# A hybrid decoder layer on one core: weight-quarter sums one product sooner, four low halves one step later, and three small steps moved inside the mixer

## The reference

```python
f = lb + (1.0 - lb) * jax.nn.sigmoid(rf)           # lb: lower bounds, a softmax over two rows
k = 1.0 - f; q = silu(rq)
o, S_new = _hgrn2_scan(q, log(f), k, ri, S0)       # S <- f*S + k i ; o = q S
p = exp(s - m) / (sum(exp(s - m)) + exp(sink - m)) # attention probabilities
x = x + _rmsnorm(concat(attention, o * silu(rg)) @ w_out, g_post_mix)
ffn = (silu(h2 @ w_gate) * (h2 @ w_up)) @ w_down   # 1024 -> 2816 -> 1024
x = x + _rmsnorm(ffn, g_post_ffn)
```

## Time and profile before

| | us |
|---|---|
| median of 3 runs | 1178.89 (1178.26 to 1178.94) |
| the profiled execution | 1179.54 |
| its span, first to last instruction | 1177.8 |
| PE busy | 1165.0 (99% of the span) |
| DVE busy | 874.2 (74%) |
| ACT busy | 533.7 (45%) |
| POOL busy | 242.2 (21%) |

### The profile page before, as it was taken

How to read it: one execution, slowest core, us unless ns; L and a number is a source line. 1 busy time by engine, 2 the same in 40 slices (tenths; PEclk the granted TensorE clock), 3 DMA queues, 4 the chain that set the end, 5 groups by cost and what they waited for, 6 DMA issues and landing times.

```text
span 1177.8 us, 22993 instructions
## 1 busy us (share of the span) xinstructions
PE 1165.0 (99%) x8962; PEld 1147.4 (97%) x8962; DVE 874.2 (74%) x1493; ACT 533.7 (45%) x1192; POOL 242.2 (21%) x190
## 2 busy tenths in 40 slices
PE   9999999999999999999999999999999999999998
PEld 9999999999999999999999999999999999999997
DVE  4988587776677747799777888888887565567676
ACT  6766656745253744564222322322322235455533
POOL 1000010201120000000232365765674020000011
PEclk9999999999999999999999999999999999999999
DMA  9521101006562243253454648766864286678446
GB/s 298 144 84 34 37 19 39 19 3 125 53 157 81 84 152 94 73 158 93 138 157 153 193 162 251 234 225 224 251 233 162 101 271 189 211 255 272 147 103 118
DMA packets 173548, 170.65 MB, mean 145 GB/s; under 512 B 23064, under 2 KB 125224, under 8 KB 172912
## 3 DMA queue, kind: packets, MB, share of 16 engines
q1 hardware_dynamic: 171264, 166.00, 46.8%
q0 software_dynamic: 2176, 3.18, 1.8%
HBM read 117.59 MB, written 52.58 MB: 144 GB/s over the span
## 4 chain that ended last, share of the span: by engine, by line
PE 86%; DVE 7%; ACT 3%; issue 2%; DMA 1%; SPq 0%; DVEq 0%; ACTq 0%
PE pair L2069 33%; PE pair L2109 17%; PE pair L1811 16%; PE pair L2028 7%; PE pair L1940 2%; PE pair L1886 1%; PE pair L2171 1%; PE pair L1901 1%; PE pair L1905 1%; DMA mix<-x_cols_dram 1%; DVE w_lo L2594 1%; PE pair L1925 1%; DVE mix L2666 1%; DMA raw<-w_in_dram 1%; PE pair L1957 1%
## 5 line engine op out<-in xcount | busy, mean ns | idle before, releaser
L2069 PE MATMUL pair<-act_hi,w_hi 128*128 128x258 f32 x704 | 199.1, 283 | 1.1 <-DVE u_tmp L2744 1.1
L2069 PE MATMUL pair<-act_lo,w_hi 128*128 128x258 f32 x704 | 198.6, 282 | 0.0
L2069 PE MATMUL pair<-act_hi,w_lo 128*128 128x258 f32 x704 | 198.6, 282 | 0.0
L2109 PE MATMUL pair<-a_ring,w_hi 128*128 128x258 f32 x1056 | 191.6, 284 | 0.5 <-DVE mix L2804 0.4
L1811 PE MATMUL pair<-act_hi,w_hi 128*128 128x344 f32 x528 | 177.0, 335 | 0.6 <-DVE act_lo L2242 0.5
L1811 PE MATMUL pair<-act_hi,w_lo 128*128 128x344 f32 x528 | 169.2, 320 | 0.0
L1811 PE MATMUL pair<-act_lo,w_hi 128*128 128x344 f32 x528 | 168.9, 320 | 0.0
L2109 PEld LDWEIGHTS pair<-a_ring,w_hi 128*128 128x128 f32 x1056 | 163.1, 189 | 1.5 <-DVE mix L2804 0.8
L1261 ACT ACTIVATE w_hi<-rawx 128x512 fp32r<-128x512 f32 (+2 forms) x97 | 68.7, 709 | 195.9 <-PE pair L2069 84.6
L2069 PE MATMUL pair<-s_hi,w_hi 128*128 128x258 f32 x528 | 149.2, 283 | 0.5 <-DVE w_lo L2594 0.5
L2069 PE MATMUL pair<-mix_r,w_hi 128*128 128x258 f32 x528 | 149.3, 283 | 0.0
(11 more groups left out here) (382 smaller groups left out, 2629.1 us busy)
## 6 DMA issues: line engine op xcount, KB each, us to landing
raw<-w_up_dram SPq DMA_DIRECT2D x26, 512.0 KB, 5.2
a_in<-h_sums SPq DMA_DIRECT2D x44, 258.0 KB, 3.3
rawx<-w_gate_dram SPq DMA_DIRECT2D x22, 512.0 KB, 5.1
w_quarter<-w_down_dram SPq DMA_DIRECT2D x44, 256.0 KB, 3.7
w_sums<-w_quarter SPq DMA_DIRECT2D x44, 256.0 KB, 4.7
rawx<-w_sums SPq DMA_DIRECT2D x44, 256.0 KB, 4.0
raw<-w_in_dram SPq DMA_DIRECT2D x18, 512.0 KB, 4.1
h_scratch<-mix SPq DMA_DIRECT2D x23, 258.0 KB, 2.1
```

The source lines that it names most:

```text
L2069: mm = pe.matmul(pair[psum_pair(n)][:, s, 0:QW], a[:, r, half + k, :], b, start=(k == 0 and i == 0), stop=(k == 3 and i == 2))
L2109: mm = pe.matmul(dpair(mt)[:, s, 0:a.shape[1]], b[:, cut], a, start=(m == 0 and n == 0), stop=(m == HALVES - 1 and n == 2))
```

## The change

Five edits; nothing is computed otherwise.

- The steps `L` of the four row sums move by one place: the first from n = 11 to 12 (behind `Y` of tile 0), the second from 12 to 13, the third from 13 to 15 (behind `Z`), the fourth from 15 to 16, behind `T4` and `W` of tile 0. The order among the four sums stays.
- For the tiles 1 to 7, `T` moves from iteration -3, where `Y` stays, to -4, counted from the tile's P6.
- The lower bounds are cut in two: three DVE instructions behind `D` of tick 27, the exponential on ACT at the end of tick 28's attention, the other five on DVE at tick 29, and a change of sign of one gain vector at tick 31.
- `R` of the one attention item that meets tick 70 moves on ACT to the end of tick 69, ahead of `unit_read`.
- On level 4 (the fifth) of heads 0 and 1, at ticks 60 and 78, DVE does the level first and `unit_finish` behind it.

```diff
 early_steps
-            8: [("S", 1, 1), ("S", 3, 1)], 9: [("X", 6), ("S", 2, 1), ("S", 4, 1)], 10: [("X", 7)], 11: [("T", 0), ("L", 2)],
-            12: [("Y", 0), ("L", 1)], 13: [("L", 3)], 14: [("T3", 0)], 15: [("Z", 0), ("L", 4)]}.get(n, [])
+            8: [("S", 1, 1), ("S", 3, 1)], 9: [("X", 6), ("S", 2, 1), ("S", 4, 1)], 10: [("X", 7)], 11: [("T", 0)],
+            12: [("Y", 0), ("L", 2)], 13: [("L", 1)], 14: [("T3", 0)], 15: [("Z", 0), ("L", 3)]}.get(n, [])
 weight_steps
-            plan = {-3: ("T", "Y"), -1: ("T3", "Z"), 0: ("T4", "W")} if q else {0: ("T4", "W")}
+            plan = {-4: ("T",), -3: ("Y",), -1: ("T3", "Z"), 0: ("T4", "W")} if q else {0: ("T4", "W")}
 shared
+    def scaled_early(tick):
+        return any(("o", h) in recurrence_steps(tick - 2) for h in range(NREC))
 scalar (ACT)
-            if tick == LB0:
-                act.wait_ge(sem("lb_step"), 1)
-                act.activation(lbt[:, 2:4, :], lbt[:, 0:2, :], ACT.Exp).then_inc(sem("lb_step"), 1)
-                elif step == "R":
+                elif step == "R" and not scaled_early(tick):
+            if tick == LB0 + 1:
+                act.wait_ge(sem("lb_step"), 1)
+                act.activation(lbt[:, 2:4, :], lbt[:, 0:2, :], ACT.Exp).then_inc(sem("lb_step"), 1)
+                    if step == "R" and scaled_early(tick + 1):
+                        unit_probabilities(i)
                 unit_read(tick // 2)
+            if n == 2 * EARLY:
+                sum_high(4)
 vector (DVE)
-        def lower_bound():
+        def bound_exponents():
             dve.wait_ge(sem("const_in"), NCONST)
             then(dve.tensor_tensor(lbt[:, 4, :], lbl[:, 0, :], lbl[:, 1, :], ALU.max))
             dve.tensor_tensor(lbt[:, 0, :], lbl[:, 0, :], lbt[:, 4, :], ALU.subtract)
             dve.tensor_tensor(lbt[:, 1, :], lbl[:, 1, :], lbt[:, 4, :], ALU.subtract).then_inc(sem("lb_step"), 1)
+
+        def lower_bound():
+
             dve.wait_ge(sem("lb_step"), 2)
-            if tick == LB0:
-                lower_bound()
-                dve.wait_ge(sem("g_in"), 16)
-                then(dve.tensor_scalar(gain[:, PRE_FFN, :], gain[:, PRE_FFN, :], -1.0, None, ALU.mult))
+            if tick == LB0:
+                bound_exponents()
+            if tick == LB0 + 2:
+                lower_bound()
+            if tick == LB0 + 4:
+                dve.wait_ge(sem("g_in"), 16)
+                then(dve.tensor_scalar(gain[:, PRE_FFN, :], gain[:, PRE_FFN, :], -1.0, None, ALU.mult))
-            levels_first = any(step[0] == "level" and step[1] >= NREC - 2 for step in recurrence_steps(tick))
+            levels_first = any(step[0] == "level" and (step[1] >= NREC - 2 or step[2] == 4) for step in recurrence_steps(tick))
+            if n == 2 * EARLY:
+                sum_low(4)
```

## The result

The changed kernel takes 1181.33 us (median of 20 runs, 1180.02 to 1182.87) against 1179.26 for the kernel before (20 runs, 1177.86 to 1181.57). The ratio is 1.0016, 95% interval 1.0010 to 1.0022 (it is not the quotient of the two medians): a little slower, by about the 0.2% that the prediction set as its bound. The forecast was 1179.8, 0.9 more than before, and too little to be told from no change. The interval leaves 1.0000 out, so 20 runs of each do tell it. The profiled execution took 1181.03 us, its span is 1179.2; the granted clock is 0.998 as before.

A forecast was written before the change was run, and what follows sets the result against it. PE is busy 99% of the span, so only its own waits count. Terms -0.30 - 0.26 + 1.15 + 0.8 - 0.45 = +0.94 us on the median 1178.89 gave 1179.8, own range 1179.0 to 1180.7, wide 1177.2 to 1181.4.

The forecast's parts named there:

- rival 4: Behind PE's new wait of 1.9 us at P3 the clock falls, costing 1.7 us: 1181.5 us; chance 0.07.
- Lower bounds: Ticks 27 to 31: DVE instructions moved behind the maximum end PE's wait at tick 28; gain 0.30, bounds -0.3 and +0.3.
- Scaling: Moving R on ACT ends PE's 0.56 wait at the transpose; -0.26 taken, the rest lost at head 1's levels.
- the 0.82: PE's level wait at 236.49 in head 1, 0.82 us, claimed to grow above 1 by the rest of the scaling gain.
- Level 4: Heads 0 and 1: unit_finish behind the level makes DVE 0.76 late; +0.4 for head 0, +0.75 for head 1.
- Low halves: Feed-forward products: u_tmp's 1.1 wait goes, but the fourth sum delays P3 to 553.7, losing 1.9; +0.8 taken.
- Weight sums: Tiles 2, 4 and 6: Y is ready some 0.7 sooner in each, ending tile 7's 0.45 wait; -0.45 taken.
- third rival: Odd tiles: POOL's instructions hold T, so PE's wait at tile 7 stays; 1180.3 us, chance 0.10.
- Rival 1: All four targeted PE waits go and nothing comes in their place: 2.5 us gained, 1176.4 us; chance 0.12.
- rival 2: Level 4 of heads 0 and 1: the order costs nothing, the shift falls into idle time; 1178.7 us, chance 0.18.

The follow-up runs named there:

- experiments 1: The changed kernel with the order of the row sums' low halves put back, all else kept: 1179.23 us, ratio 1.0003 to the kernel before.
- 2: The changed kernel with the level test put back, so unit_finish stands ahead of level 4 again: 1178.99 us, ratio 0.9996 to the kernel before.
- 6: The kernel before with only the level edit (level ahead of unit_finish at level 4 of heads 0 and 1): 1180.52 us, ratio 1.0012.
- the repeat: The changed kernel, unaltered, timed once more: 1181.70 us, ratio 1.0023 to the kernel before.
- experiments 3: The third order: the changed kernel with low halves of the third sum ahead of Z, the fourth ahead of T4 and the reading before it: 1178.73 us, ratio 0.9998.
- 4: The changed kernel with the level test put back and the low halves in the third order: 1177.09 us, ratio 0.9982 to the kernel before.

## Why the prediction was right, point by point

The sum was +0.94 and the columns give +1.03 (without the start and the stretch that no edit touches). That the two are so near is partly luck: three terms were 30 to 43% too small, two of them gains (0.52 together) and one a loss (0.49). And the median is not as near as the sum: 1181.33 lies above the forecast's own range (1179.0 to 1180.7), at the end of the wide one (1181.4), next to rival 4's 1181.5, though the clock didn't fall behind P3. Of the 1.5 us between it and 1179.8, 0.37 is that the kernel before had 1179.26 in 20 runs and 1178.89 in the three of the forecast; most of the rest is in no term and no column ("What stays open"). So that it still lies in the wide range is luck; what came out is the mechanism of each edit but one, and their sum in the traces.

- **Lower bounds**, forecast -0.30, measured -0.53. The mechanism was right. The size was not: the listed wait is not all that PE loses at it (below).
- **Scaling**, forecast -0.26, measured -0.25: right in size by luck, wrong in place. "The rest is added to the 0.82" failed. PE wins 0.78 at the transpose and gives 0.38 and 0.14 back at two score matmuls ahead of the level, in ticks 72 and 76. In the changed kernel:

```profile
213.93 0.19 ACT L1460 ACTIVATE esk<-tsum 128x2 f32<-128x2 f32 x1
...
214.15 0.16 DVE L2458 TENSOR_TENSOR den<-den,esk 128x2 f32<-128x2 f32 x1 [3.94 <-ACT esk L1460]
...
215.41 0.31 PE L1818 MATMUL pair<-act_hi,w_lo 128*128 128x344 f32 x1
215.55 0.16 DVE L2454 TENSOR_TENSOR tsum<-sink,negm 128x2 f32<-128x2 f32 x1
215.85 0.47 PE L1893 MATMUL pair<-k_hi,q_hi 128*128 128x512 f32 x1
...
236.86 1.13 PE L1947 MATMUL pair<-hqk,mix 128*128 128x128 f32 x8 [0.81 <-issue]
```

  DVE stands 3.94 for ACT's exponentials ahead of `den`, and the maximum (tsum) comes behind `den`, so it comes no sooner. The forecast had said itself that "the next exponential comes no sooner", and did not follow it one step on, to the maximum and the next scores. 215.41 and 215.85 are 0.44 apart where matmuls of that shape follow each other by 0.16.
- **Level 4**, forecast +1.15, measured +1.64. Head 1 was +0.75 forecast, +0.76 measured. Head 0 was +0.4 and is 0.88: the first score matmul loses 0.55 (it was put at 0.32), and a second one, at 186.60, 0.33. "The following scores meet the same shift" had named that second one and priced it at 0.08. This is the worst-sized term.
- **Low halves**, forecast +0.8, measured 2.32 - 1.41 = +0.91. P3 was forecast at 553.7; it started at 554.82 with PE 1.16 behind the kernel before ahead of this stage, which is 553.66 on the clock of before. Counting DVE's queue instruction by instruction, from rows of one kernel, gave P3's start to within 0.1 us over 18 us. A part of that is chance: on the same clock DVE's pair ended at 553.5 in place of 553.7, and PE started 0.14 behind it, which the count had left out. The two halves of the term were both too small, 1.1 for a gain of 1.41 and 1.9 for a loss of 2.32.
- **Weight sums**, forecast -0.45, measured -0.74. The lead does add up over the even tiles and tile 7's wait goes. Beside POOL the third rival's mechanism is there. T of tile 7 in the changed kernel:

```profile
638.43 1.63 DVE L2616 TENSOR_TENSOR t<-raw 128x512 f32<-128x512 f32 x1
639.47 1.75 POOL L1221 TENSOR_TENSOR mix<-mix,e_buf 128x516 f32<-128x516 f32 x1
640.10 1.67 DVE L2617 TENSOR_TENSOR t<-raw,t 128x512 f32<-128x512 f32 x1
```

  In the kernel before, the first of the two came at the end of POOL's instruction ahead of that one (L1216, 639.40 to 640.70):

```profile
640.55 0.70 DVE L2603 TENSOR_TENSOR t<-raw 128x512 f32<-128x512 f32 x1
```

  It took 0.70 there. Now it starts 0.22 behind the start of that instruction (now L1219, 638.21 to 639.51), takes 1.63 and ends 0.55 behind it; the second ends at 641.77, 0.55 behind POOL's instruction, as it did in the earlier trace rows. The rule that the prediction cited (the Trainium skill, page "SBUF — State Buffer", section "SBUF: two separate sides") agrees with that: T moved into POOL's preceding instruction, and won nothing. The rival's conclusion, that the wait at tile 7 stays, fell all the same, because three even tiles bring enough.
- **The other rivals.** Rival 1 (nothing new is late) and rival 2 (level order free) are out by experiments 1, 2 and 6. For rival 4, the window around the new wait:

```profile
554.00:558.00 4.00, 3.18 (x26) 3.21 (x27) 3.78 (x6) 0.70 (x1) 0.00 (x0) 1.00 0.26 73
```

  The granted clock is 1.00 behind a wait of 2.03 between full work; it did not fall.

**What stays open.** The columns say 1.03 to 1.06, the two profiled executions differ by 1181.03 - 1179.54 = 1.5 (0.28 of it is the start), the medians by 2.1, and by 2.6 in the repeat. So 1.0 us, and 1.6 in the repeat, stand in no column: about half of what was measured, or more. For the six other kernels that were run more than once the ratio gives 0.1 to 0.6 us more than the columns (for the third order without its 1.64), and the ratios' intervals, about 1 us to either side, cover that. For the changed kernel they don't, either time. What differs from one execution to the next is seen in the table (the start by up to 0.9, the clock near 320 by 1.6 once). A longer fall of the clock does not explain it: on the chip of the repeat its three runs with a granted clock of 0.998 took 1180.45 to 1180.90, and the nine of the kernel before with the same clock 1178.19 to 1179.25. Each kernel has one or two traces, and where the rest goes is not explained.

## What to carry to other kernels

When an edit moves work behind the instruction that PE waits for, count the queue of that engine on to the next two readers of what was moved: the start of P3 in the changed kernel could be told from the trace before to 0.1 us, and the order that keeps the gain (experiments 3 and 4) came from the same count. If an engine waits for a second engine right behind the moved step, putting the step later wins nothing: it turns into idle time ahead of that wait and is paid again behind it. And a gain has to be followed past the next instruction of the engine that didn't get faster.

## What the runs showed of the hardware that was not expected

A listed wait of PE is less than what PE loses by it. The entries of the earlier trace rows against the shift of PE at the same place: 0.30 listed and 0.53 lost, 0.45 and 0.73, 0.56 and 0.78, 1.13 and 1.40; new in the changed kernel 0.31 and 0.55, 2.03 and 2.2 to 2.3. It is 0.2 to 0.3 more each time. The rows of tick 62 above show where it is: matmuls of 0.32 start 0.16 apart, so their listed ends overlap, and a wait, which counts from the end of the last one, leaves that 0.16 out (179.19 to 179.82 is 0.63, of which 0.31 is listed). And the first matmul after the stop takes 0.31 to the next, where the same shape takes 0.23. So in these traces a wait counts as its listing plus about 0.24 wherever PE had been running without a gap; where it already stood a little, as at level 6 of head 1 (0.81 listed, 0.76 more than before), it does not. Added to the forecast's terms, this one correction takes -0.30 to -0.54 and -0.45 to -0.69, and head 0 from 0.32 + 0.08 to 0.56 + 0.32, all within 0.05 of what was measured. It was read from these same waits, so that is no test of it.
